# One program for the opening and the first projections of a two-block transformer kernel

## The reference

```python
mod = jax.nn.silu(c) @ w_ada[l] + b_ada[l]
sh1, sc1, g1, sh2, sc2, g2 = jnp.split(mod[:, None, :], 6, axis=-1)
h = modulate(rmsnorm(x, norm_mix_g[l]), sh1, sc1)     # h * (1 + sc1) + sh1
proj = h @ w_in                                       # 1024 x 4888
```

## Time and profile before

| | |
|---|---|
| median of three runs | 1815.24 us |
| lowest and highest | 1815.1 and 1817.8 us |
| span of the profiled execution, the only time that its page gives | 1813.6 us |
| busy in that span | PE 1691.4 us (93%), DVE 804.5, ACT 543.4, POOL 50.2 |

### The profile page before, as it was taken

The page is one execution under the profiler, slowest core; times in us unless marked ns, Lnnn a source line. Parts: engine busy times, 40 slices in busy tenths (PEclk is TensorE's granted clock), DMA queues, the critical chain, the costliest instruction groups (busy, mean ns, idle before and its releaser), DMA issues. The chain is left out here.

```text
span 1813.6 us, 20133 instructions
## 1 busy us (share of the span) xinstructions
PE 1691.4 (93%) x8179; PEld 1175.6 (65%) x8179; DVE 804.5 (44%) x1240; ACT 543.4 (30%) x899; POOL 50.2 (3%) x89
## 2 busy tenths in 40 slices
PE   2999999889999999999999999998999988988988
PEld 2788766668878888888788876766344343433446
DVE  4764467654642232365622464245243232322345
ACT  4312356742362222232532450423100000000036
POOL 0000010100000000000000000000200000000000
PEclk9989999989999999999999999999999999999999
DMA  9775310002613333221422021247899999999961
GB/s 349 234 255 166 140 70 1 2 23 94 232 47 94 107 107 110 81 94 47 162 93 93 1 93 47 96 179 305 309 426 423 427 426 426 426 426 426 426 248 47
DMA packets 87798, 351.74 MB, mean 194 GB/s; under 512 B 9926, under 2 KB 39282, under 8 KB 71577
## 3 DMA queue, kind: packets, MB, share of 16 engines
q1 hardware_dynamic: 85146, 346.08, 49.4%
q0 software_dynamic: 2560, 4.37, 0.7%
HBM read 346.03 MB, written 8.43 MB: 195 GB/s over the span
## 5 line engine op out<-in xcount | busy, mean ns | idle before, releaser
L572 DVE TENSOR_TENSOR arena<-ring,arena 128x1024 fp32r<-128x1024 f32 x120 | 146.9, 1225 | 229.5 <-ACT arena L621 206.4
L2876 PE MATMUL ex_h<-ring,u_big_tail 128*64 128x512 f32 x512 | 153.8, 610 | 15.0 <-DMA ring<-in_w 8.0
L577 PE MATMUL up_ps<-h_high,arena 128*128 128x512 f32 x352 | 138.0, 392 | 2.6 <-DVE arena L572 2.5
L578 PE MATMUL up_ps<-arena 128*128 128x512 f32 x352 | 137.6, 391 | 0.0
L579 PE MATMUL up_ps<-h_high,arena 128*128 128x512 f32 x352 | 137.5, 391 | 0.0
L621 ACT CAST arena<-ring 128x1024 fp32r<-128x1024 f32 x81 | 84.9, 1048 | 149.3 <-PE up_ps L579 82.1
L2876 PE MATMUL ex_h<-s_ab,u_big_tail 128*64 128x512 f32 x272 | 116.1, 603 | 1.5 <-DVE u_big_tail L2847 1.5
L2876 PEld LDWEIGHTS ex_h<-ring,u_big_tail 128*64 128x64 f32 x512 | 47.1, 140 | 80.3 <-issue 79.3
L3154 ACT ACTIVATE u_big_tail<-ex_h 128x512 f32<-128x512 f32 x16 | 9.6, 597 | 298.0 <-PE ex_h L2876 297.9
L2847 DVE TENSOR_TENSOR u_big_tail<-ex_x,vcol 128x512 f32<-128x512 f32 x32 | 20.6, 686 | 175.9 <-PE ex_x L2840 175.9
L2876 PE MATMUL ex_h<-w1flat,u_big_tail 128*64 128x512 f32 x160 | 73.5, 608 | 6.5 <-DMA s_ab<-in_w 6.5
(11 more groups left out here) (596 smaller groups left out, 3629.3 us busy)
## 6 DMA issues: line engine op xcount, KB each, us to landing
ring<-in_w SPq DMA_DIRECT2D x42, 2048.0 KB, 32.8
s_ab<-in_w SPq DMA_DIRECT2D x32, 2048.0 KB, 31.4
ring<-in_w_in SPq DMA_DIRECT2D x19, 2048.0 KB, 8.1
ring<-in_w_ada SPq DMA_DIRECT2D x24, 1024.0 KB, 6.9
reg_a<-in_w SPq DMA_DIRECT2D x10, 2048.0 KB, 31.8
w1flat<-in_w SPq DMA_DIRECT2D x10, 2048.0 KB
ring<-in_w_ffn_gate SPq DMA_DIRECT2D x11, 1024.0 KB, 5.4
ring<-in_w_ffn_up SPq DMA_DIRECT2D x11, 1024.0 KB, 8.6
```

The costliest lines, as they stand in the source:

```text
L572: return engine.tensor_tensor(lo, v, hi.bitcast(F32), ALU.subtract)
L577: nc.tensor.matmul(ps, x[0], y[0], start=start, stop=False)
L578: nc.tensor.matmul(ps, x[0], y[1], start=False, stop=False)
L2876: mm = nc.tensor.matmul(ps[half, :], xT[:, k, half], ws[j][:, k, cols], start=(k == 0), stop=(k == k_end - 1))
```

## The change

- The opening and the projections become one program, with no barrier between them.
- SP loads c first, as 128 short runs of 8 elements and straight into its columns. Pieces 0 to 2 follow, then x in four tiles with a semaphore each, then pieces 3 to 7. The chunk behind them is cut in two: its first half (columns 0 to 255) has a semaphore of its own.
- The nine small vectors and `g_ffn_2` are issued by ACT, on its own DMA queue, after silu. DVE waits for their turned columns ahead of piece 3, no longer at its start.
- The last piece is summed in four quarters of the columns, in the order 0, 2, 1, 3, and PE adds up each quarter when it is there, now with 64 columns of ones, into two banks: feature tiles 0 to 3 are complete after two quarters.
- Shift and multiplier, the modulation of h and its splitting go tile by tile, on DVE and ACT in turns, with the splits of units 0, 1 and 2 in between.
- PE works on units 0 and 1 together: of each feature tile, three matmuls of the one and three of the other. Unit 1 has a third pair of buffers.
- PE's wait for piece 5 is gone; saving h and clearing the region now wait by semaphores for what they need.

```diff
+            b.ch.arrived[0] -= 16
+            b.ch.landed[-1] -= 16
+            b.first_part = b.c_in[0]
+        else:
+            b.c_in.append(add(feature_tiles(w, ends[j], ends[j + 1]), region=j % 2))
     def modulation():
...
-BY_ROWS = ["g_ffn_2", "c"]
+BY_ROWS = ["g_ffn_2"]
...
-    vrow = b.scr[0:NV, 0:P]
+    ROWS = NV - KD
+    vrow = b.s_ab[0:ROWS, 16 * U:16 * U + P]
...
+    QUARTERS = (0, 2, 1, 3)
...
+    b.begin_program()
+    block = b.block
...
+        b.ps_sum = [ps_ctx.enter_context(nc.psum_tensor(f"op_c{i}", [P, CH], F32)) for i in range(2)]
...
+            return b.ps_sum[n % KD // 4][:, (n // KD * 4 + n % 4) * 64:(n // KD * 4 + n % 4 + 1) * 64]
...
-            sp.dma_start(b.x[:], a["x"][0].rearrange("(t p) d -> p t d", p=P)).then_inc(x_in, 16)
-            for name, k in VROWS:
...
+            sp.dma_start(c_col, a["c"].rearrange("a (p k) -> (a p) k", p=P)).then_inc(c_in, 16)
             for k in range(KD):
+                if k == 3:
+                    for t in range(NT):
+                        sp.dma_start(b.x[:, t, :], a["x"][0, t * P:(t + 1) * P, :]).then_inc(x_in[t], 16)
                 sp.dma_start(piece(k), b.ada1[:, k, :]).then_inc(landed[k], 16)
...
-            nc.tensor.transpose(psv[:, 0:NV], vrow, b.ident[0:NV, 0:NV]).then_inc(cols, 1)
+            nc.tensor.transpose(psv[:, 0:ROWS], vrow, b.ident[0:ROWS, 0:ROWS]).then_inc(cols, 1)
             pe.wait_ge(cols_out, 1)
-            nc.tensor.matmul(psc[:, 0:2 * KD], b.ident[:], bias[:, 0:2 * KD], start=True, stop=False, skip_group_check=True)
-            pe.wait_ge(landed[5], 16)
+            for i in range(2):
+                for half in range(2):
+                    nc.tensor.matmul(b.ps_sum[i][:, half * 256:half * 256 + 256:64], b.ident[:],
+                                     bias[:, half * KD + 4 * i:half * KD + 4 * i + 4],
+                                     start=(half == 0), stop=False, skip_group_check=True)
...
-            pe.wait_ge(added, KD)
-            for n in range(2 * KD):
-                mm = nc.tensor.matmul(psc[:, n:n + 1], acc[:, n * P:n * P + P], b.ones[:, 0:1],
-                                      start=False, stop=(n == 2 * KD - 1), skip_group_check=True)
-            mm.then_inc(summed, 1)
+            for i, q in enumerate(QUARTERS):
+                pe.wait_ge(added, KD + i)
+                for n in range(4 * q, 4 * q + 4):
+                    mm = nc.tensor.matmul(column(n), acc[:, n * P:n * P + P], b.ones[:, 0:64],
+                                          start=False, stop=(n % KD % 4 == 3 and n >= KD), skip_group_check=True)
+                if i % 2:
+                    mm.then_inc(summed, 1)
...
-            dve.wait_ge(cols, 1)
-            nc.vector.tensor_copy(b.vcol[:], psv[:, 0:NV]).then_inc(cols_out, 1)
...
                 if k == 3:
+                    dve.wait_ge(cols, 1)
+                    nc.vector.tensor_copy(b.vcol[:, 0:ROWS], psv[:, 0:ROWS]).then_inc(cols_out, 1)
                     dve.wait_ge(squared, 1)
...
+                elif k < KD - 1:
+                    dve.wait_ge(added, k)
...
                 else:
...
+                    for q in QUARTERS:
+                        cols_q = slice(q * CH, q * CH + CH)
+                        nc.vector.scalar_tensor_tensor(out=acc[:, cols_q], in0=piece(k)[:, cols_q], scalar=by, in1=acc[:, cols_q],
+                                                       op0=ALU.mult, op1=ALU.add).then_inc(added, 1)
...
-            dve.wait_ge(summed, 1)
...
-            act.wait_ge(cols_out, 1)
-            nc.scalar.activation(b.sc[:], b.vcol[:, VAT_ROWS + KD:VAT_ROWS + 2 * KD], ACT.Silu).then_inc(silu, 1)
-            act.wait_ge(x_in, 16)
+            act.wait_ge(c_in, 16)
+            nc.scalar.activation(b.sc[:], c_col, ACT.Silu).then_inc(silu, 1)
+            for name, k in VROWS:
...
+                act.dma_start(vrow[r:r + KD, :], a[name].rearrange("a (p k) -> (a k) p", p=P)).then_inc(loads, 16)
             for t in range(NT):
+                act.wait_ge(x_in[t], 16)
                 last = nc.scalar.activation(y[:, t, :], b.x[:, t, :], ACT.Square, accum_out=ss[:, t:t + 1])
...
-            act.wait_ge(mul, 1)
...
-        return self.w[u % 2][part][:].rearrange("p (k n) -> p k n", k=v.shape[1])
+        if self.third is not None:
+            w = self.third[part] if u == 1 else self.w[(u - 1) % 2 if u else 0][part]
+        else:
+            w = self.w[u % 2][part]
...
-        if u >= 2:
+        if self.third is not None and u in (2, 3):
+            if u == 3:
+                act.wait_ge(self.used, 1)
+        elif u >= 2:
             act.wait_ge(self.used, u - 1)
...
+            v = b.chunk(b.c_in[c], n0 // FIRST)[:, :, n0 % FIRST:n0 % FIRST + P] if c == 0 else b.chunk(b.c_in[c])[:, :, n0:n0 + P]
+            units.append((FIRST_PART if c == 0 and n0 < FIRST else b.c_in[c], v, False))
...
+    third = nc.alloc_sbuf_tensor_at("p1_third", [P, 4 * U], F32R, offset=b.s_ab_at + 12 * U * 4)
...
+            sp.wait_ge(b.ev_a, KD // 2)
+            sp.wait_ge(b.ev_d, KD // 2)
             sp.dma_start(b.h_dram, b.hTflat[:]).then_inc(b.h_saved, 16)
...
+        def first_two(pe):
...
+            for k in range(KD):
+                for u in range(2):
+                    if k == 0:
+                        pe.wait_ge(parts.lo, u + 1)
+                    if u == 0:
+                        pe.wait_ge(parts.h_lo, k + 1)
+                    mm = product_parts(nc, ps[u][:], [parts.unit(u, j)[:, k, :] for j in range(2)],
+                                       [parts.h[j][:, k, :] for j in range(2)], k == 0, k == KD - 1)
+                    if k == KD - 1:
+                        mm.then_inc(parts.used, 1)
...
-                if kind in ("q", "T", "dup"):
+                if i == 0:
+                    first_two(pe)
+                elif i == 1:
+                    pass
...
+            first = 3 if i == 0 else until(i - 1)
...
-            return len(units) if tiles[i][2] == "wide" else min(unit_of[i] + 2, len(units))
+            if i < 2:
+                return 3 + i
+            return len(units) if tiles[i][2] == "wide" else max(4, min(unit_of[i] + 2, len(units)))
...
+            pool.wait_ge(b.ring_used[3], 1)
             nc.gpsimd.memset(b.acc2, 0.0).then_inc(cleared, 1)
...
+        def columns(dve, i):
...
+            ks = slice(4 * i, 4 * i + 4)
+            dve.wait_ge(b.summed, i + 1)
+            nc.vector.tensor_copy(b.modcol[:, 0:2 * KD].rearrange("p (h k) -> p h k", h=2)[:, :, ks],
+                                  b.ps_sum[i][:, 0:CH:64].rearrange("p (h k) -> p h k", h=2)).then_inc(b.mod, 1)
...
+            nc.vector.scalar_tensor_tensor(out=b.mulcol[:, ks], in0=b.modcol[:, KD + 4 * i:KD + 4 * i + 4], scalar=1.0,
...
+        def affine_even(dve, k):
+            dve.wait_ge(b.raw, k + 1)
+            nc.vector.tensor_scalar(b.hT[:, k, :], b.hT[:, k, :], b.mulcol[:, k:k + 1], b.modcol[:, k:k + 1],
+                                    ALU.mult, ALU.add).then_inc(b.ev_d, 1)
...
+        def low_h(dve, k):
+            dve.wait_ge(parts.h_hi, k + 1)
+            lower(nc.vector, parts.h[1][:, k, :], b.hT[:, k, :], parts.h[0][:, k, :]).then_inc(parts.h_lo, 1)
...
+        def affine_odd(act, k):
+            act.wait_ge(b.mul, k // 4 + 1)
+            act.wait_ge(b.raw, k + 1)
+            nc.scalar.activation(b.hT[:, k, :], b.hT[:, k, :], ACT.Identity, scale=b.mulcol[:, k:k + 1],
+                                 bias=b.modcol[:, k:k + 1]).then_inc(b.ev_a, 1)
...
+        def high_h(act, k):
+            act.wait_ge((b.ev_d, b.ev_a)[k % 2], k // 2 + 1)
+            nc.scalar.copy(parts.h[0][:, k, :], b.hT[:, k, :]).then_inc(parts.h_hi, 1)
...
+            columns(dve, 0)
+            affine_even(dve, 0)
             parts.dve_w(dve, 0)
-            parts.dve_h(dve)
+            low_h(dve, 0)
+            affine_even(dve, 2)
+            parts.dve_w(dve, 1)
+            low_h(dve, 1)
+            low_h(dve, 2)
+            columns(dve, 1)
+            affine_even(dve, 4)
+            low_h(dve, 3)
+            affine_even(dve, 6)
+            for k in range(4, KD):
+                low_h(dve, k)
+            parts.dve_w(dve, 2)
...
             parts.act_w(act, 0)
-            parts.act_h(act)
+            parts.act_w(act, 1)
+            for k in range(0, KD, 2):
+                affine_odd(act, k + 1)
+                high_h(act, k)
+                high_h(act, k + 1)
+            parts.act_w(act, 2)
```

More of the change, by code:

```diff
@@ L233, in load_until @@
             for part, dram in enumerate(self.ch.items[i]):
-                sp.dma_start(self.chunk(i, part), dram).then_inc(self.ring_full[r], 16)
+                first = i == self.first_part and part == 0
+                sp.dma_start(self.chunk(i, part), dram).then_inc(self.first_in if first else self.ring_full[r], 16)
         self.loaded = max(self.loaded, min(end, len(self.ch.items)))
@@ L331, in stage_modulation @@
```

(31 more changed lines are left out.)

42 lines of the change are left out of this document (19 added, 23 removed).

## The result

The kernel after the change took 1823.41 us (median of 12 runs, 1818.0 to 1825.45), the kernel before beside it 1816.61 (12 runs, 1812.61 to 1819.04). The ratio is 1.0038 with a 95% interval of 1.0029 to 1.0047: some 6.8 us slower, above the 0.2% named as the limit. The forecast was 1809.9, and its range ended at 1813.0. The profiled execution has a span of 1821.6 us, 8.0 more than before.

A forecast was written before the change was run, and what follows sets the result against it. The opening was taken to bound the kernel: the first two units would end at 54.1 instead of 60.4 (6.3 us saved), or 56.0 at low clock (4.4). Middle 5.3: 1815.24 - 5.3 = 1809.9, range 1802.8 to 1813.0.

The forecast's parts named there:

- POOL's clearing: Opening, behind piece 7: POOL clears for 3.5 us, from 39 to 42, listed as moved without cost.
- the clock: PE's dense start: full clock saves 6.3 us, a low stretch as long as before 4.4; middle taken, 5.3.
- The small vectors on ACT's queue: Opening loads: packets alternate with SP's, 85 of ACT's per engine; vectors land at 24.9, piece 3 starts at 26.6.
- from 33.8 on it is slower beyond the noise: Landing time of the small vectors from which the kernel would be measurably slower; the gain would be gone at 30.2.
- DVE's sum, the norm, the column sums, the tile-by-tile part: Opening from piece 3 at 26.6: column sums from 36.9, three matmuls at 42.2, the other 45 from 43.9.
- Interleaving: Units 0 and 1 on PE: doubles work per feature tile, so splits no longer hold PE; saves no matmul.
- Later parts move with the opening: Behind the opening: the rest moves forward as a whole, the first expert gather as much earlier as the eviction.
- whole loads take turns: Rival, DMA queues: one load's share on an engine is a turn; vectors near 40, slower, 1825; chance 0.06.
- vectors early, 1804.0: Rival, opening: vectors come early, x decides, piece 3 at 19.9, dense start at 38.0; saving 11.2; chance 0.36.

The follow-up runs named there:

- experiment 3: Changed kernel with 64 of 128 positions of all eight `g_ffn_2` rows as single elements, the rest contiguous; 1817.27 us, taken once.
- 4: Changed kernel with four of eight `g_ffn_2` rows as single elements, 128 on each of four engines, the rest contiguous; 1824.03 us, taken once.
- 1: Changed kernel with `g_ffn_2` loaded straight into its columns as 128 runs of 8 elements, still on ACT's queue; 1806.34 us, ratio to before 0.9933.
- 6: Changed kernel with all small loads on SP's queue, behind c and ahead of the pieces, `g_ffn_2` still by single elements; 1810.55 us, ratio to before 0.9978.
- Experiment 2: Changed kernel with POOL's clearing also waiting for the last rest of h, slow load kept; 1820.69 us, ratio to before 1.0015.
- Experiment 8: Against 5: PE does unit 0 and then unit 1, not interleaved; 1806.32 us, ratio to before 0.9951.
- 11: Against 5: the last piece summed in one instruction instead of four quarters; 1805.58 us, ratio to before 0.994.
- 5: Changed kernel with both `g_ffn_2` loaded straight into its columns and POOL's clearing behind the last rest of h; 1806.53 us, ratio to before 0.9951.
- Experiment 7: Kernel before with only c and `g_ffn_2` loaded straight into their columns; 1813.26 us, ratio to before 0.9991.
- 9: Against 5: five unread matmuls of 512 columns on PE between the column sums and unit 0; 1809.3 us, ratio to before 0.9967.
- 10: Against 5: column sums with one column of ones instead of 64; 1806.18 us, ratio to before 0.9944.

## Why the prediction was wrong, point by point

By its own steps, in the profiled executions: the forecast had the second eviction at 54.1 to 56.0, middle 55.05, and it came at 68.12, 13.1 later. The parts are 9.1 for the vectors (piece 3 at 35.73, forecast 26.6), 2.9 for POOL's clearing (3.36, forecast 0.48) and 1.0 for the clock (the low end, not the middle), 13.0 in all.

- *The small vectors on ACT's queue: the step that failed.* The mechanism held: packets in turns, DVE idle behind the transposed rows, one wait deciding the sum. The term was mis-sized. It counted "64 single elements of `g_ffn_2`" for an engine, 85 packets in all; the load sits on eight engines with 128 each, 149 in all. The vectors were to land at 24.9 and landed at 34.5, and piece 3 started at 35.73 instead of 26.6. The count is 6.2 us of this: with half the elements on each engine (experiment 3) they landed at 28.4. The other 3.5 us would have been missed with the right count too; about 2 of them (an estimate) are the start of ACT's queue, whose first packets ran behind 6 us and not at 4, and for the rest no run gives a cause. Experiments 3 and 4 show that the number on one engine decides, 1 and 6 that it needs both the single elements and the full queue beside them. The text's own threshold ("from 33.8 on it is slower beyond the noise") was passed, by 0.7 us. By itself this term makes the kernel 3.8 us slower (9.1 less the 5.3 to be gained), just beyond the noise; with the next one it is 6.7.
- *POOL's clearing, costed at nothing: the second fault.* It was placed rightly, behind piece 7, and only its transfers and the save were looked at, not which instruction of DVE it falls beside. It had lain beside subtractions, which bore it; it was moved beside a scaling, which took 2.8 us more (3.36 for 0.53). Experiment 2 gives 2.6 us in the trace and 2.7 in the medians.
- *The clock* took the low one of the two ends: it was low from 52.0 to 58.8, across the start of the dense part, and from first product (54.38) to second eviction were 13.7 us, where the forecast had 13.8 at the low end and 11.9 at the full clock.
- *DVE's sum, the norm, the column sums, the tile-by-tile part* were right in their sum: from piece 3 to the first product 18.65 us, or 15.8 without POOL's 2.9, where the forecast had 15.6. The sums were to cost "at least nothing" more than 5.05 and took 3.79, because the row behind the 5.05 was read as if at one clock: in the kernel before the clock fell at 37.7, 2.1 us into the sums. They also started 0.5 us later behind piece 3 than forecast (10.8 for 10.3), so the good sum is in part two small errors that cancel.
- *Interleaving*: "no longer held by the splits" was credited as the reason why the dense part runs at PE's pace. Experiment 8 shows no gain from it, with PE at the low clock for most of unit 0; what it does at the full clock no run shows.
- *Later parts move with the opening*: right. Gather +7.26, span +8.0, second eviction +7.67.
- *The rivals.* None had this mechanism with this size. The one that ended slower (whole loads take turns) had the right consequence, a landing between 32 and 40, for a wrong reason: turns are single packets (24 to 32 of ACT's in every microsecond), not the 9 to 17 descriptors that the forecast quotes for it. That its time was nearest is luck. The first (vectors early, 1804.0) is what experiment 1 makes of the kernel; it took 1806.34. Its steps hold: piece 3 at 19.52 (19.9 in the text), the cast behind the half chunk at 32.24 (32.2), the first product at 38.17 (38.0), though the last by luck, since 1.83 of it is POOL's stall.

With the two terms put right the sum is 1815.24 - 5.3 + 9.1 + 2.9 = 1821.9 against 1823.41 measured beside a kernel before that stood at 1816.61: a difference of +6.7 against +6.8. In the profiled executions the clock's 1.0 comes on top, and +7.7 is what the second eviction shows.

The version to keep is 1, or 11: each 10.8 us under the kernel before that ran beside it, and some 17 under after. In the traces of before and 1 this gain has two parts of like size. The column sums start 5.2 us earlier (30.36 for 35.57), which the loads give, and some 1.5 of it the quarters (11 against 5). From there to the first product it takes 7.81 us instead of 11.83, another 4.0, with POOL's stall still inside; that is the joined program with its splitting tile by tile, and 1.3 of it is the sums at full clock. Experiment 7, the direct load without all this, gained 0.76 at the second eviction, where 1 gained 9.15. The order of the loads, the joined program and the tile-by-tile part were not taken out one at a time.

## What to carry to other kernels

Count a small load's packets on its busiest DMA engine, not over all of them, before it is put beside a queue that is never empty: here each packet cost a packet of the other queue, and a load of 4 KB in single elements came later than 10 MB. When a step of POOL is moved, look at which kind of DVE instruction it comes to lie beside, not only at who waits for it. Once one wait is gone, look for the next one that ends last: here it was the landing of the first half chunk, and it hid what the sums gained. And a microsecond gained ahead of PE's dense work may be taken back by its clock (1.83 us in 5), so an edit is worth what the medians say and not what the first product says.

## What was not expected of the hardware

- A load of 1024 single elements on ACT's queue needed from its issue at 6.3 to 34.5 us beside the stream, and was in at 8.26 ahead of it.
- A POOL memset of 4096 columns (3.51 us) held a DVE scaling of 512 columns until it was over (3.36 instead of 0.53) and left a subtraction of 1024 columns untouched (1.23).
- 32 sums with one column of ones took longer than with 64 (5.42 and 3.79 us), only because the clock fell at 32.1 in between; in before (37.7) and 7 (33.8) it fell on one-column sums too.
- The clock, low for 3.4 us in one version and 6.8 in another that started its dense part 1.8 us earlier, evened the two out. Near 1720 it fell in 9, 10 and 11 and not in 1, 5 and 8, whatever it had done in the opening.
